# Second attention of a two-block network: the product with the values next to the following head's scores, and query tiles next to the turn of the exponents

## The reference, cut to what matters

```python
for g, (window, dilation) in enumerate(DILATED_PAIRS):
    q = apply_rope_2(q_all[:, :, g], cos, sin)
    o_g, lse_g = dilated_window_attention(q, k_shared, v_shared, window, dilation)
alpha = jax.nn.softmax(jnp.stack(lses, axis=0), axis=0)
merged = jnp.sum(alpha[..., None] * jnp.stack(outs, axis=0), axis=0)
x = x + (merged * jax.nn.silu(gate)) @ w_out_b[i]
```

## Time and profile before

| | |
|---|---|
| median of 3 runs | 2401.69 us (2400.87 to 2401.92) |
| the profiled execution | 2401.36 us, span 2399.6 us |
| PE busy in the span | 2370.3 us (99%) |
| DVE busy | 1599.2 us (67%) |
| ACT busy | 1124.4 us (47%) |
| mean granted TensorE clock | 0.999 |
| first scores of the second attention | 1977.18 us |
| last O of the second attention | 2291.31 us |

### The profile page before, as it was taken

The page is one execution under the profiler, slowest core; times in us unless marked ns, Lnnn a source line. Parts: engine busy times, 40 slices in busy tenths (PEclk is TensorE's granted clock), DMA queues, the critical chain, the costliest instruction groups (busy, mean ns, idle before and its releaser), DMA issues.

```text
span 2399.6 us, 31111 instructions
## 1 busy us (share of the span) xinstructions
PE 2370.3 (99%) x10980; PEld 1969.3 (82%) x10980; DVE 1599.2 (67%) x1950; ACT 1124.4 (47%) x1415; POOL 9.8 (0%) x18
## 2 busy tenths in 40 slices
PE   6999999999999999999999999999999999999998
PEld 6888788888888888888888888888888888888887
DVE  7998899999787765445444464545655557777664
ACT  4544545544464444444444454445544444444554
POOL 0001000000000000000000000000000000000000
PEclk9999999999999999999999999999999999999999
DMA  9985479999858875555655655665555554454454
GB/s 392 379 314 199 152 260 352 333 337 364 313 192 270 285 251 182 194 185 192 207 195 194 192 188 184 207 202 186 198 188 192 184 192 158 145 171 153 158 192 158
DMA packets 148490, 539.32 MB, mean 225 GB/s; under 512 B 16768, under 2 KB 18080, under 8 KB 147744
## 3 DMA queue, kind: packets, MB, share of 16 engines
q1 hardware_dynamic: 145584, 528.28, 64.0%
q10 hardware_dynamic: 2800, 9.59, 1.1%
HBM read 535.69 MB, written 2.11 MB: 224 GB/s over the span
## 4 chain that ended last, share of the span: by engine, by line
PE 95%; DVE 2%; issue 1%; DMA 1%; ACT 1%; SPq 0%; ACTq 0%; DVEq 0%
PE acc L1860 29%; PE acc L1862 29%; PE acc L1861 29%; PE tb L1942 2%; PE tb L2341 1%; DVE macc L1272 1%; PE acc L1912 0%; PE acc L1910 0%; PE acc L1911 0%; PE tb L2344 0%; PE tb L2073 0%; PE tb L1860 0%; PE tb L1862 0%; PE tb L1861 0%; DVE lo L1100 0%
## 5 line engine op out<-in xcount | busy, mean ns | idle before, releaser
L1100 DVE TENSOR_TENSOR lo<-raw,hi 128x1024 fp32r<-128x1024 f32 (+1 forms) x812 | 972.5, 1209 | 597.2 <-ACT hi L536 594.5
L536 ACT ACTIVATE hi<-raw 128x1024 fp32r<-128x1024 f32 (+1 forms) x812 | 845.9, 1049 | 899.5 <-PE acc L1862 725.3
L1860 PE MATMUL acc<-hi,Hh 128*128 128x512 f32 x1968 | 778.5, 396 | 2.1 <-DVE Hl L1592 0.7
L1862 PE MATMUL acc<-hi,Hl 128*128 128x512 f32 x1968 | 767.3, 390 | 0.0
L1861 PE MATMUL acc<-lo,Hh 128*128 128x512 f32 x1968 | 766.2, 389 | 0.0
L1860 PEld LDWEIGHTS acc<-hi,Hh 128*128 128x128 f32 x1968 | 369.6, 188 | 80.5 <-issue 5.7
L1862 PEld LDWEIGHTS acc<-hi,Hl 128*128 128x128 f32 x1968 | 369.3, 188 | 78.2
L1861 PEld LDWEIGHTS acc<-lo,Hh 128*128 128x128 f32 x1968 | 369.8, 188 | 75.8 <-issue 1.4
L1860 PE MATMUL acc<-hi,hbh 128*128 128x512 f32 x512 | 204.8, 400 | 0.0
L1862 PE MATMUL acc<-hi,hbl 128*128 128x512 f32 x512 | 200.1, 391 | 0.0
L1861 PE MATMUL acc<-lo,hbh 128*128 128x512 f32 x512 | 199.6, 390 | 0.0
(11 more groups left out here) (307 smaller groups left out, 1924.3 us busy)
## 6 DMA issues: line engine op xcount, KB each, us to landing
raw<-in_wa_dram SPq DMA_DIRECT2D x680, 512.0 KB, 4.3
late_raw<-in_wa_dram SPq DMA_DIRECT2D x96, 512.0 KB, 5.5
raw<-in_wb_dram SPq DMA_DIRECT2D x96, 512.0 KB, 3.6
start_raw<-in_wa_dram SPq DMA_DIRECT2D x64, 512.0 KB, 6.9
raw<-in_wc_dram SPq DMA_DIRECT2D x64, 512.0 KB, 3.4
x<-in_x_dram SPq DMA_DIRECT2D x2, 1024.0 KB, 6.1
gm<-gate_rows ACTq DMA_DIRECT2D x2, 1024.0 KB, 8.3
x<-in_x_dram ACTq DMA_DIRECT2D x1, 2048.0 KB, 8.5
```

The costliest lines, as they stand in the source:

```text
L536: act.activation(hi[:, s, 0:n], raw[:, r, 0:n], ACT.Copy).then_inc(hi_ready, 1)
L1100: dve.tensor_tensor(lo[:, s, 0:n], raw[:, r, 0:n], hi[:, s, 0:n].bitcast(F32), ALU.subtract)\
L1860: pe.matmul(dst(tt), a, hi[:, s, w], start=first and i == 0, stop=False)
L1862: mm = pe.matmul(dst(tt), b, hi[:, s, w], start=False, stop=last and i == kts - 1)
```

## The change

The products with the values move from four to six units behind the head's scores, which is the unit after which the next head's scores come; they are called ahead of them. Only the last head keeps its place. They write bank 3 of `tb` in place of bank 2, and DVE reads and frees bank 3. The query tiles at j = 13 and 19 are turned after j = 14 and 20, where a K stands too (in blocks 1 to 3), and Q is called ahead of K. DVE's and ACT's lists are as before, but for the numbers that they take from the table: `take_queries` follows `QUERIES_AT`.

```diff
-QUERIES_AT = {n: QB + 24 * (n // 3) + (13, 19, 27)[n % 3] for n in range(Q_TILES)}
+QUERIES_AT = {n: QB + 24 * (n // 3) + (14, 20, 27)[n % 3] for n in range(Q_TILES)}
 SCORES_AT = {h: QB + 24 * (h // Q_HEADS + 1) + 5 + 6 * (h % Q_HEADS) for h in range(HEADS2)}
+OUTPUTS_AT = {h: SCORES_AT[h + 1] if h < HEADS2 - 1 else SCORES_AT[h] + 4 for h in range(HEADS2)}
...
                 split_to(SCORES_AT[head] + 4 + 4)
                 dve.wait_ge(o_ready, c.up("o"))
                 for tt in range(TT):
-                    ins = dve.tensor_scalar(O2[:, tt, cols(head * HD, HD)], tb[:, 2, tt * P:(tt + 1) * P], resum[:, tt:tt + 1],
+                    ins = dve.tensor_scalar(O2[:, tt, cols(head * HD, HD)], tb[:, 3, tt * P:(tt + 1) * P], resum[:, tt:tt + 1],
                                             None, ALU.mult)
-                ins.then_inc(tb_free[2], 1)
+                ins.then_inc(tb_free[3], 1)
...
             def output(head):
-                taken(3)
-                fill(2)
+                fill(3)
                 vh = lambda tt: v2[:, tt, head * HD:(head + 1) * HD]
-                pe.matmul(tb[:, 2, 0:HD], pt2[:, T:T + P], vh(0), start=True, stop=True)
-                pe.matmul(tb[:, 2, HD:2 * HD], pt2[:, 0:P], vh(0), start=True, stop=False)
-                pe.matmul(tb[:, 2, HD:2 * HD], pt2[:, P:T], vh(1), start=False, stop=True).then_inc(o_ready, 1)
+                pe.matmul(tb[:, 3, 0:HD], pt2[:, T:T + P], vh(0), start=True, stop=True)
+                pe.matmul(tb[:, 3, HD:2 * HD], pt2[:, 0:P], vh(0), start=True, stop=False)
+                pe.matmul(tb[:, 3, HD:2 * HD], pt2[:, P:T], vh(1), start=False, stop=True).then_inc(o_ready, 1)
...
                 for head in range(HEADS2):
-                    if unit == SCORES_AT[head] + 3:
-                        key_major(head)
-                    if unit == SCORES_AT[head] + 4:
+                    if unit == OUTPUTS_AT[head]:
                         output(head)
                 for n in range(Q_TILES):
                     if unit == QUERIES_AT[n]:
                         turned_queries(n)
+                for head in range(HEADS2):
+                    if unit == SCORES_AT[head] + 3:
+                        key_major(head)
                 for head in range(HEADS2):
                     if unit == SCORES_AT[head]:
                         scores(head)
```

## The result

The changed kernel takes 2412.47 us (median of 6, 2412.19 to 2412.81) against 2400.95 us before: a ratio of 1.0047 with a 95% interval of 1.0037 to 1.0057, 11.5 us slower. The forecast was 2413.5.

A forecast was written before the change was run, and what follows sets the result against it. PE bounds the kernel, never waiting in the changed stretch. Waits of 14.0 us less 2.0 of switches give +12.0 on 2401.36, 2413.4, stated as 2413.5 us; range 2403 to 2419, likeliest case 2409 to 2418 (chance 0.70).

The forecast's parts named there:

- PE never waits before, so waits are new costs: In the changed stretch PE is busy 80.30 of 80.30 us, so time moves only by shorter PE work or new waits.
- The chain behind O(h1): Blocks 1 to 3, j = 17: late `rotate`, splits and softmax delay K(h2) by 3.1 us each, 9.3 us in all.
- the 0.26 us from the end of a DVE instruction to PE's start: Assumed lag at every PE wait on DVE: 673.35 + 0.69 = 674.04 to 674.30 us.
- PE's own path to K(h2): Without waits, PE would reach K(h2) 11.57 us after O(h1) starts: 5.34 + 5.44 + 0.79.
- The chains behind O(h2) and O of the last head: Late splits after `rotate` delay PE 1.2 us in blocks 1 to 3 (3.5 us), 0.5 in blocks 2 and 3 (1.0).
- The K called on time by 0.08 us: K(h3) and its like, 7 places: possible start 10.70 us after O, PE arrives at 10.78, so no wait.
- Block 4: Gated tiles replace rotations: K(h2) can start at 11.92 us against PE's 11.71, a wait of 0.2 us.
- Switches, 2.0 us: On PE, fewer excursions from the products save 1.2 + 0.1 + 0.7 = 2.0 us, bounds 1.4 and 2.5.
- O in front of S: Values products directly ahead of scores save 0.06 to 0.13 us for 12 heads, 0 to 0.07 for three.
- K behind Q: Query turn directly ahead of K saves one resumption, 0.12 us, in 6 places, two in each of blocks 1 to 3.
- Loads covered: SP's loads land 3.6 us after a split, ACT wants them three PE units later: covered, no added time.
- The rival with 1.2 GHz: PE's clock falls in 6 waits of 1.2 us and more, costing 20 us more: 2433 us, chance 0.03.

The follow-up runs named there:

- attended_follows: Changed kernel with `attended` two units later in DVE's list and query tile 3b+1 (block 4: gated tile) ahead of attended(h1): 2400.23 us, ratio 0.9995.

## Why the prediction was right

- *PE never waits before, so waits are new costs.* Right: all of the 11.7 us are waits on DVE, and with DVE's list in order the time is before's.
- *The chain behind O(h1).* Right to 0.3 us in what it costs (3.1 forecast, 2.8 measured) and to 0.2 in its times: K(h2) at 14.68 us after O forecast, 14.47 measured; unit 19 at 6.85 forecast, 6.64 measured. The step that was mis-sized is the 0.26 us from the end of a DVE instruction to PE's start, taken from the earlier trace rows: the sums end at 2113.41 + 1.26 = 2114.67 and K starts at 2114.73, 0.06 us later, and it is 0.05 or 0.06 at unit 19, at Q and at unit 11 too. In the feed-forward part the load of the weights ahead of the product starts only at 674.27, and the trace puts that down to "issue" and not to DVE; what held it there is not known. Eight places at 0.2 us are most of the 2.3 us between 14.0 forecast and 11.7 measured; PE's own path to K(h2), 11.69 us and not 11.57, is 0.4 of it.
- *The chains behind O(h2) and O of the last head.* Right in place and kind, 1.2 forecast and 0.9 measured, 0.5 and 0.3. The K called on time by 0.08 us were so, by 0.38: the sums end 10.44 us after O as worked out, K(h3) comes at 10.82, and the release is shorter. A block from scores to scores was to take about 84.7 us and takes 84.1.
- *Block 4.* 0.2 us forecast, under 0.1 seen: the sums for K(h2) end at 2278.54 + 1.27 = 2279.81 and K starts at 2279.87, at the very edge of a wait.
- *Switches, 2.0 us.* Too high, 1.1 us in attended_follows and under 1 in the changed kernel. O in front of S saves 2.72 - 2.66 = 0.06 us, the lower of the two bounds that the rows gave. K behind Q costs 1.24 us where the two cost 0.36 and 0.89 to 0.93: 0.01 to 0.05 and not 0.12, since K starts 0.87 us after Q and not 0.79. The term that was mis-sized took the whole slow resumption as saved where K meets Q, and nearly twice the saving of O in front of S.
- *The total.* Waits were 2.3 us too high and the saving at least 0.9 too high. The two errors have opposite signs in the sum, so that the total, 11.8 us over the median that it started from against 11.5 measured, is closer than its terms by luck. The other 0.7 us between 2413.5 and 2412.47 is the starting point: 2401.69 from three runs, 2400.95 from six.
- *Loads covered.* Right in effect and wrong in the step: ACT did wait for loads, 15.7 us in 7 places in the stretch, since a late split delays the load into the same place of the ring. After the split that ended at 2138.85, ACT stood 2.90 us and could round at 2142.45, 3.6 us behind the split, which is the time that a load takes. PE has no wait for ACT or for loads.
- *The clock.* It stayed at 1.00 in the stretches with waits, and products after a wait were as far apart as before. The rival with 1.2 GHz did not come. The Trainium skill, "TensorE: Matmul & The Clock Gate" (part 1), says that the gate follows how busy PE has been; here waits of up to 1.2 us did not bring the lower clock.

## What to carry to other kernels

When a producer's step is moved later, look at what stands behind its consumer in the consumer's own list: the wait itself may be free (DVE stood 76 us here), and the work queued behind it is what comes late. Count the slack first: here one unit was free to the last tenth, the second cost 11 us, and moving the consumer's step by as much as the producer's, with the tile that does not need it put ahead, gave it all back. Merging excursions on PE (putting one step that interrupts the products directly beside another) paid little in this kernel: 0.06 us for the product with the values ahead of the scores (both float32 matmuls), 0.01 to 0.05 for K behind Q (both transposes) and nothing for K ahead of the scores. And measure a tile added in SBUF by itself: one that moved the tiles of the weights cost more than anything else tried here, and the same tile laid behind all others cost nothing that can be seen.

## What was not expected of the hardware

The address of the tile that a float32r product takes its weights from sets the rhythm of the products: 227 ns apart at the old addresses, 233 ns with these tiles 32 or 64 bytes further on, 232 to 233 ns with 128, at the same granted clock (0.999) and with nothing waiting. A spare tile of 32 bytes makes the whole kernel 2.3% slower, nearly five times as much as the change of this study. Why the address counts, and which addresses are good ones, these runs do not show. And K's three transposes hold PE 0.33 us ahead of the scores' float32 matmuls and 0.25 ahead of products: these 0.08 us are most of the 0.12 that merging was to save.
